# Block-diagonal state products, a 128-row gate product and another order of mask and outputs in a hybrid decoder layer

## What is computed

```python
g = jax.nn.log_sigmoid((a_glr @ gla_w_gate[l] + gla_b_gate[l]).astype(jnp.float32)) / GLA_GATE_TEMP   # a_glr: rank 16
...
def step(state, inp):                      # one chunk of tokens; the state is 48 x 96 for each head
    qb, kb, vb, gb = inp
    b = jnp.cumsum(gb, axis=2)
    o_inter = jnp.einsum('bhik,bhkv->bhiv', qb * jnp.exp(b), state)
    ...
    scores = jnp.einsum('bhik,bhjk,bhijk->bhij', qb, kb, decay)
    o_intra = jnp.einsum('bhij,bhjv->bhiv', scores, vb)
    b_last = b[:, :, -1]
    k_dec = kb * jnp.exp(b_last[:, :, None, :] - b)
    state = jnp.exp(b_last)[..., None] * state + jnp.einsum('bhjk,bhjv->bhkv', k_dec, vb)
    return state, o_inter + o_intra
```

## Time and profile before

| | |
|---|---|
| median of three runs | 2469.27 us |
| profiled execution, span | 2474.4 us |
| granted TensorE clock, mean | 0.988 |
| TensorE busy | 2397.1 us (97%) |
| TensorE weight loads busy | 1924.9 us (78%) |
| VectorE busy | 1696.9 us (69%) |
| ScalarE busy | 1134.8 us (46%) |
| GpSimd busy | 961.9 us (39%) |
| mean DMA rate | 153 GB/s |

### The profile page before, as it was taken

How to read it: one execution, slowest core, us unless ns; L and a number is a source line. 1 busy time by engine, 2 the same in 40 slices (tenths; PEclk the granted TensorE clock), 3 DMA queues, 4 the chain that set the end, 5 groups by cost and what they waited for, 6 DMA issues and landing times.

```text
span 2474.4 us, 33363 instructions
## 1 busy us (share of the span) xinstructions
PE 2397.1 (97%) x11866; PEld 1924.9 (78%) x11866; DVE 1696.9 (69%) x2479; ACT 1134.8 (46%) x2012; POOL 961.9 (39%) x768
## 2 busy tenths in 40 slices
PE   7999999999999998999899999999999999999997
PEld 6777777777678876777788888788778878887885
DVE  7455457676356775455778888768978888886655
ACT  6534254332146664324444444444654444445444
POOL 1111003342055872223456555333445555651211
PEclk9999999899999998999999999999999999999999
DMA  4332325444497426355223233497532232227764
GB/s 179 111 102 92 103 78 171 135 154 130 168 322 250 135 67 234 120 221 223 103 107 111 107 115 115 150 304 244 176 122 103 108 121 104 110 95 260 228 193 143
DMA packets 190116, 378.16 MB, mean 153 GB/s; under 512 B 17136, under 2 KB 61184, under 8 KB 180736
## 3 DMA queue, kind: packets, MB, share of 16 engines
q1 hardware_dynamic: 189952, 376.04, 44.7%
HBM read 252.00 MB, written 123.98 MB: 152 GB/s over the span
## 4 chain that ended last, share of the span: by engine, by line
PE 49%; DVE 7%; ACT 2%; issue 2%; DMA 1%; SPq 0%; POOL 0%; ACTq 0%; DVEq 0%; POOLq 0%
PE ff_bank L78 14%; PE ff_bank L80 14%; PE ff_bank L79 14%; PE op_bank L70 2%; PE op_bank L72 2%; PE op_bank L71 2%; DVE ff_y_gate L2947 2%; DVE ff_ring L2960 2%; DVE ff_ring L2908 1%; DVE ff_b_lo L2902 1%; ACT ff_y_gate L2748 1%; DMA op_mix_in<-mix_t 0%; ACT ff_ring L2763 0%; ACT ff_e L2725 0%; DVE ff_u L2929 0%
## 5 line engine op out<-in xcount | busy, mean ns | idle before, releaser
L79 PE MATMUL ff_bank<-ff_b_lo,ff_ring 128*128 128x512 f32 x1232 | 480.8, 390 | 0.0
L78 PE MATMUL ff_bank<-ff_b_hi,ff_ring 128*128 128x512 f32 x1056 | 416.7, 395 | 18.0 <-ACT ff_e L2725 11.6
L80 PE MATMUL ff_bank<-ff_b_hi,ff_ring 128*128 128x512 f32 x1056 | 412.7, 391 | 0.0
L70 PE MATMUL ip_bank<-ip_x_hi,ip_w_hi 128*128 128x512 f32 x736 | 307.2, 417 | 12.7 <-DVE ip_x_lo L721 12.7
L71 PE MATMUL ip_bank<-ip_x_lo,ip_w_hi 128*128 128x512 f32 x736 | 290.5, 395 | 0.0
L72 PE MATMUL ip_bank<-ip_x_hi,ip_w_lo 128*128 128x512 f32 x736 | 289.9, 394 | 0.0
L79 PEld LDWEIGHTS ff_bank<-ff_b_lo,ff_ring 128*128 128x128 f32 x1232 | 232.0, 188 | 47.5 <-issue 0.5
L78 PEld LDWEIGHTS ff_bank<-ff_b_hi,ff_ring 128*128 128x128 f32 x1056 | 199.0, 188 | 74.5 <-issue 29.0
L78 PE MATMUL ff_bank<-ff_ring,ff_ring 128*128 128x512 f32 x616 | 242.4, 394 | 6.0 <-DVE ff_ring L2960 6.0
L80 PE MATMUL ff_bank<-ff_ring,ff_ring 128*128 128x512 f32 x616 | 240.4, 390 | 0.0
L79 PE MATMUL ff_bank<-ff_ring,ff_ring 128*128 128x512 f32 x616 | 240.3, 390 | 0.0
(11 more groups left out here) (317 smaller groups left out, 4957.6 us busy)
## 6 DMA issues: line engine op xcount, KB each, us to landing
ff_raw<-in_slabs SPq DMA_DIRECT2D x44, 1024.0 KB, 4.8
proj_t<-ip_staged SPq DMA_DIRECT2D x92, 256.0 KB, 2.8
a_t<-ff_y_val SPq DMA_DIRECT2D x44, 512.0 KB, 2.6
t_t<-ff_t_sum SPq DMA_DIRECT2D x88, 256.0 KB, 2.0
ff_raw_ring<-t_t SPq DMA_DIRECT2D x56, 256.0 KB, 3.9
ff_raw_ring<-s_t SPq DMA_DIRECT2D x52, 256.0 KB, 3.3
rp_tables<-in_rope SPq DMA_DIRECT2D x24, 512.0 KB, 4.5
ff_raw_ring<-in_w_down SPq DMA_DIRECT2D x46, 256.0 KB, 3.5
```

What stands on the lines that cost most here:

```text
L70: pe.matmul(out, w_hi[k], x_hi[k], start=(k == 0), stop=False)
L78: pe.matmul(out, w_hi, x_hi, start=first, stop=False, skip_group_check=resumed)
L79: pe.matmul(out, w_hi, x_lo, start=False, stop=False, skip_group_check=resumed)
L80: return pe.matmul(out, w_lo, x_hi, start=False, stop=last, skip_group_check=resumed)
```

## The change

- The output of a pair of heads is one block: the two scores products write their halves of one output of 192 columns, and one product of the pair's 128 rows of `q_start` with a 128 x 192 `state` that is block-diagonal adds both heads' state parts. The output of pair m lies in `s_bank[m]`, and ScalarE copies 192 columns in a row.
- `state` holds two blocks of 96 columns for each pair, zeroed once in full. `gl_advance` updates each head's block on its own 64 rows: four instructions in place of two.
- The gate product runs over all 128 rows of the tile that holds the gate inputs: `low_rank` is loaded with 128 rows, and `w_gate` is zero on the other 112.
- `gl_mask(j)` moves from the head of iteration GL_AT+1 to iteration GL_AT, behind `drain(n)` and ahead of `turn_pairs(n)`.
- On TensorE the output of pair 0 stands behind step GL_AT+1, that of pair 1 behind piece 0 of step GL_AT+2; none stands within step GL_AT+1.
- The scan of the gates takes the tile of ones, and a constant with its load goes. Some tiles lie elsewhere.

```diff
-        low_rank = placed("gl_low_rank", [RANK, 2, CH], 7168)
+        low_rank = placed("gl_low_rank", [P, 2, CH], 7168)
-        state = placed("gl_state", [P, 2, GP, DV], 27136)
-        w_gate = placed("gl_w_gate", [RANK, GP, P], 28672)
-        starts = placed("gl_starts", [P, CH], 29696)
+        state = placed("gl_state", [P, 2, GP, 2, DV], 27136)
+        w_gate = placed("gl_w_gate", [P, GP, P], 31232)
...
-                sp.dma_start(low_rank[:, j % 2, :], proj_t[T_AQ, GLR_ROW:GLR_ROW + RANK, at]).then_inc(low_loaded[j % 2], 16)
+                sp.dma_start(low_rank[:, j % 2, :], proj_t[T_AQ, :, at]).then_inc(low_loaded[j % 2], 16)
...
-                    ins = act.activation(o_all[:, j % 4, :].rearrange("p (m b v) -> p m b v", m=GP, b=2)[:, :, b, :],
-                                         s_bank[b][:, GP * CH:GP * (CH + DV)].rearrange("p (m v) -> p m v", m=GP), ACT.Copy)
+                    ins = act.activation(o_all[:, j % 4, 2 * b * DV:2 * (b + 1) * DV], s_bank[b][:, GP * CH:GP * (CH + DV)], ACT.Copy)
...
-                    dve.tensor_tensor_scan(cum[:, m, :], starts[:, :], z[:, m, :], 0.0, ALU.mult, ALU.add).then_inc(cum_ready, 1)
+                    dve.tensor_tensor_scan(cum[:, m, :], ones[:, :], z[:, m, :], 0.0, ALU.mult, ALU.add).then_inc(cum_ready, 1)
...
-                    ins = dve.scalar_tensor_tensor(out=state[:, (j + 1) % 2, m, :], in0=state[:, j % 2, m, :], scalar=e_end[:, j % 2, m:m + 1],
-                                                   in1=st_bank[:, m * DV:(m + 1) * DV], op0=ALU.mult, op1=ALU.add)
+                    for b in range(2):
+                        rows = slice(64 * b, 64 * (b + 1))
+                        ins = dve.scalar_tensor_tensor(out=state[rows, (j + 1) % 2, m, b, :], in0=state[rows, j % 2, m, b, :],
+                                                       scalar=e_end[rows, j % 2, m:m + 1],
+                                                       in1=st_bank[rows, m * DV:(m + 1) * DV], op0=ALU.mult, op1=ALU.add)
...
-                    if n == GL_AT[j] + 1:
-                        gl_mask(j)
...
                     drain(n)
+                if n in GL_AT:
+                    gl_mask(GL_AT.index(n))
                 if is_rope(n):
                     turn_pairs(n)
...
-            def gl_output(j, h):
-                if h == 0:
+            def gl_output(j, m):
+
+                if m == 0:
...
-                m, b = h // 2, h % 2
-                out = s_bank[b][:, GP * CH + m * DV:GP * CH + (m + 1) * DV]
-                pe.matmul(out, scores[:, h, :], v_tok[:, h * DV:(h + 1) * DV], start=True, stop=False)
-                ins = pe.matmul(out, q_start[64 * b:64 * b + DK, j % 2, m, :], state[64 * b:64 * b + DK, j % 2, m, :],
-                                start=False, stop=True)
-                if h == GH - 1:
+                out = s_bank[m][:, GP * CH:GP * (CH + DV)]
+                for b in range(2):
+                    h = 2 * m + b
+                    pe.matmul(out[:, b * DV:(b + 1) * DV], scores[:, h, :], v_tok[:, h * DV:(h + 1) * DV], start=b == 0, stop=True,
+                              skip_group_check=b > 0)
+                ins = pe.matmul(out, q_start[:, j % 2, m, :], state[:, j % 2, m, :, :].rearrange("p b v -> p (b v)"),
+                                start=False, stop=True, skip_group_check=True)
+                if m == GP - 1:
...
                     project(n, 0, 1)
-                    gl_output(GL_AT.index(n - 2), 2)
-                    project(n, 1, 2)
-                    gl_output(GL_AT.index(n - 2), 3)
-                    done = 2
+                    gl_output(GL_AT.index(n - 2), 1)
+                    done = 1
                 if n - 1 in GL_AT:
                     project(n, done, 6)
                     gl_update(GL_AT.index(n - 1))
-                    project(n, 6, 7)
-                    gl_output(GL_AT.index(n - 1), 0)
-                    done = 7
+                    done = 6
...
                 if n - 1 in GL_AT:
-                    gl_output(GL_AT.index(n - 1), 1)
+                    gl_output(GL_AT.index(n - 1), 0)
```

More of the change, by code:

```diff
@@ L598, in gl_gate @@
                 if j == 0:
-                    act.wait_ge(gl_consts_in, 16 * 6)
+                    act.wait_ge(gl_consts_in, 16 * 5)
                 else:
@@ L822, in gl_zero @@
                 dve.memset(scores[:, :, :], 0.0).then_inc(gl_zeroed, 1)
-                dve.memset(state[:, 0, :, :], 0.0).then_inc(gl_zeroed, 1)
+                dve.memset(state[:, :, :, :, :], 0.0).then_inc(gl_zeroed, 1)
                 dve.wait_ge(gl_zeroed, 2)
-                dve.wait_ge(gl_consts_in, 16 * 6)
+                dve.wait_ge(gl_consts_in, 16 * 5)
             def halves(x):
@@ L3135, in mixer_constants @@
 def mixer_constants():
-    starts = np.ones((P, CH), np.float32)
-    starts[:, 0] = 0.0
     j = np.arange(P)[:, None]
     i = np.arange(CH)[None, :]
-    return {"starts": starts, "causal": np.ascontiguousarray(np.broadcast_to((i >= j)[:, None, :], (P, 2, CH))).astype(np.uint32)}
+    return {"causal": np.ascontiguousarray(np.broadcast_to((i >= j)[:, None, :], (P, 2, CH))).astype(np.uint32)}
 def program(nc, t, out_t):
@@ L3230 @@
     arrays["w_in"] = flat(w.reshape(KT, P, TILES, P).transpose(2, 1, 0, 3))
-    arrays["gla_w_gate"] = flat(pad_heads(a["gla_w_gate"][0]).reshape(RANK, GP, P))
+    gla_w_gate = np.zeros((P, GP * P), np.float32)
+    gla_w_gate[GLR_ROW:GLR_ROW + RANK] = pad_heads(a["gla_w_gate"][0])
+    arrays["gla_w_gate"] = gla_w_gate.reshape(P, GP, P)
     arrays["gla_b_gate"] = per_channel(pad_heads(a["gla_b_gate"][0]))
```

20 lines of the change are left out of this document (10 added, 10 removed).

## The result

In the first comparison, four runs of each kernel, the changed kernel took 2455.61 us (2450.63 to 2455.95) and the kernel before 2467.92: a ratio of 0.9939, with an interval of 0.9923 to 0.9954. It is faster, by 12 us where 33 to 35 were forecast. Two later comparisons, on two different chips and with longer series of the kernel before, gave 0.9893 (0.9876 to 0.9910) and 0.9897 (0.9875 to 0.9919), so by its comparisons the change is worth between 12 and 25 us, and by none of them what was forecast.

What follows compares the result with a forecast made beforehand. TensorE, busy for 97% of the span, was taken as the bound. Outputs -26.9, gate -4.9, stall and clock -8.2, new stalls +1.5 make -38.5 us; the middle between 2430.8 and 2437.6 gave 2434, range 2424 to 2444, with rivals to 2456.

Steps and rivals of the forecast that it cites:

- The product term: TensorE's output products, paired over 128 rows, save 26.9 us, and the gate product over 128 rows saves 4.9 us.
- The stops: On TensorE, products over fewer than 128 rows stop the pipeline on entry and leaving; one head's output costs 0.79 us.
- The second rival: Pipeline stops are the state product's own, not due to row count: a pair costs 1.17 us, time 2453, chance 0.05.
- The scores' wait and the clock behind it: TensorE's 1.42 us stall for masked scores at 472.21 and 6.8 us lost at half clock both go: 8.2 us.
- VectorE's room in the rope part: Projections 56 to 79: VectorE needs 154.4 of TensorE's 170.8 us, so only 1.5 us of new short stalls.
- cost of the mask itself unchanged: Mask moved earlier on VectorE: same cost, waiting for the scores 0.5 us at most, 0.8 behind three transposes.
- The first rival: VectorE becomes the bound in the rope part, its 32.6 us of waits for ScalarE staying: about 2449 us, chance 0.13.
- The slow rival: Early mask delays rope chain and drains, 8.2 us per stall in nine chunks: five give 2475, nine 2508; chance 0.05.

Runs made afterwards that it cites:

- the third: The kernel before, unchanged, profiled a third time: span 2470.8 us, stretch from projection 45 to 89 347.6 us.
- the second and the fourth execution: The changed kernel, not altered further, profiled again: spans 2451.9 and 2447.3 us, stretch from projection 45 to 89 323.0 and 322.8 us.

## Why the prediction was off

**The product term held, a little smaller.** 31.8 us were predicted for outputs and gate. A pair measured 0.79 us, not 0.74: by the single records of this block the state product's second pass starts 0.19 us behind the first where 0.16 was put, and the steps of the small passes are 0.11 where 0.107 was; the 0.40 from there to the second projection pass is what was put (0.16 + 0.24). That makes 32 x (1.58 - 0.79) = 25.3 us in place of 26.9. The gate came out at 0.46 (0.45 predicted). Two of the nine gates that stand alone, those of the first two chunks, lie ahead of the stretch (at 271.4 and 283.5 us), so in the stretch the sum is 26.9 + 4.1 = 31.0 predicted and 25.3 + 4.1 = 29.4 by the measured pair. The stretch, with waits and lost clock taken out on both sides (349.2 - 1.9 - 6.85 = 340.5 before; 321.4 - 7.6 - 1.7 = 312.1 after), shows 28.4 us. The gap lies in what was taken out, not in the passes: the early mask alone (341.6 with 0.5 of wait and no half clock) and the run without the cosine product (311.0 with neither) need hardly any correction, and they differ by 30.1.

**The stops belong to the row count.** The pair's state product over 128 rows starts without one and is left in 0.22 us. The second rival is refuted. The Trainium skill (TensorEngine Tiling (Array Packing), Key Properties) says that a switch between tiling modes drains TensorE. If a product over 16 or 48 rows is such a mode, the rows agree, and this case prices it: 0.84 us for four passes over 16 rows, 0.46 for the same over 128.

**The scores' wait and the clock behind it went**, as predicted, and the early mask alone takes them away (the run of the mask alone: 7.6 us, predicted 8.2). The blocks alone, with the mask in its old place, have no such wait either; their first output stands later. So each of the two edits does by itself what the forecast put down to both. The half-clock piece was no accident of the one execution: it stood in the kernel before again (13.7 us, then 10.2 in the third) and in the one with the gate alone.

**The step that failed is "VectorE's room in the rope part"**, its 1.5 us for new stalls. Measured are 7.6 us of waits, 6.7 of them for the normalised output, and 3.4 us at half clock behind the worst of them (6.8 in the second and the fourth execution, in two pieces). Two things were wrong in it. I asked only whether drains would be late and how much slack they have the earlier trace rows; no drain was late in any run. The order on VectorE sets a second date, the normalised output that TensorE transposes behind a step, and its slack was never read. It stood in the trace of the kernel before: the output was ready only 0.05 to 0.06 us ahead of its transposes in two of the sixteen chunks and 0.64 in a third, where the worst drain had 2.05. One of the two:

```profile
473.83 1.65 DVE L913 TENSOR_TENSOR gl_o_n<-gl_o_all,gl_rstd 128x384 f32<-128x384 f32 x1
```

```profile
475.53 0.76 PE L1108 MATMUL ip_bank<-gl_idf,gl_o_n 128*128 128x128 f32 x3
```

This is the larger part: with the mask back, or behind the shuffle, 5.2 and 5.3 us of the waits remain, and with the product ahead of the shuffle they end. And I costed the moved mask at nothing ("cost of the mask itself unchanged"), which is true of the mask and not of its neighbours: VectorE's work came to 164.8 us where 154.4 was put, and with the mask behind the shuffle it is 157.1, so 7.7 of the 10.4 are the cover that was lost beside GpSimd. That part is worth about 2.3 us of the waits, and the half clock.

**The first rival** had the right engine and the wrong place: VectorE did cost a part of the gain, through its order and the price of its instructions beside GpSimd, not through the waits for ScalarE's gate chain. These fell, as the row of L831 has them, from 32.6 us to 5.0:

```profile
L831 DVE SCALAR_TENSOR_TENSOR gl_z<-gl_z,gl_z_abs 128x256 f32<-128x256 f32 x8 | 7.0, 880 | 5.0 <-ACT gl_z_abs L612 4.9
```

**The slow rival** had the right suspect. The early mask does cost, 4 to 6 us of the stretch where TensorE is fast (323.0 to 317.2 with it behind the shuffle, 321.4 to 317.1 with it back). But it costs by taking cover away, not by standing at its own wait (0.3 us in the nine chunks of the rope part), and no drain was held.

**The account.** 38.5 us were predicted for the span, 0.8 of them (two gates) ahead of the stretch and 37.7 in it. Short of that in the stretch: 2.6 in the products (31.0 put, 28.4 shown), 6.1 in waits (7.6 where 1.5 was put), 1.7 in clock; 0.5 came on top, since all 1.9 us of the old wait went where 1.42 was counted. 37.7 - 2.6 - 6.1 - 1.7 + 0.5 = 27.8, the stretch's 349.2 - 321.4. Ahead of it 0.5 us were gained, and 7.7 were lost behind step 89, in the same code: 20.6, the difference of the spans. Of the 7.7, 5.0 are time in which TensorE stood (1843.5 - 1776.6 against 1835.8 - 1773.9, by the rows above), and 6.9 us more at half clock, half of it lost, make up to 3.4 of the rest. This last piece is the part that no reading of the change could give.

Why the comparisons differ isn't shown. The kernel before ran at 2467.9 in the first (four runs) and at 2472.9 to 2476.2 in the three longer series, the changed one at 2448.1 to 2455.6. The time behind step 89 moves by as much from one execution to the next, but the three longer series ran on three different chips, and only one execution of each has a profile.

**What it is worth once mended.** With the mask behind the shuffle and the normalising product ahead of it the stretch is 312.7, with two updates 312.3, against 309 to 312 forecast. The stretch is shorter by 36.9 us, the ratio to before is 0.9859, and the medians are 33.4 us apart: what was forecast for the change comes with another order of mask and normalising product and two updates in place of four.

## What to carry to other kernels

When an engine becomes faster, list every product that it takes from each other engine and read the slack of each, not only of the one that was tight before. Moving an instruction on VectorE also moves what stands behind it against GpSimd's work: put there what GpSimd doesn't hold up (here the mask that reads PSUM) and keep products of two SBUF inputs, and here the copy too, away from it. And before a difference of half a per cent is explained, compare the times of the code that didn't change: here they moved by 8 us between executions of one and the same kernel.

## What the runs showed of the hardware

- Beside GpSimd's products of 128 x 512 and 128 x 1024 a VectorE product of 128 x 256 took 1.51 and 2.11 us, and 0.41 where none ran. Such products and scans that started beside one ended 0.28 us behind its end, 17 of 17 in the changed kernel's rope part. A copy of 128 x 2 took 0.16 us alone and 1.13 to 1.26 beside one, though it is a one-input instruction. The masked copy out of PSUM took 0.43 us either way.
- Four updates of 64 rows that alternate between row halves took 1.29 us, two of 128 rows and twice the columns 0.73.
- A pair's four f32 passes of 96 columns over 128 rows start 0.105 us apart, as the 128-column transposes in the earlier trace rows do, and not the 0.08 that the prediction worked out for 96 columns.
- A wait of TensorE of 3.5 us was followed by 3.4 us at a granted clock of 0.51, one of 1.25 us before by 13.7 at 0.50: the longer stop had the shorter piece at half clock behind it. Waits of 2.2 and 2.3 us (mask back, mask behind the shuffle) had none at all.
